# A hybrid attention layer on one core: rotated half tiles split into high and low parts, joined by 64 small transfers, and x by rows loaded behind a weight chunk

## What is computed

```
u    = rms_norm(x, attn_pre_g)
proj = u @ w_in                      # 1024 x 1952: MLA latents (416), then MoBA q, k, v (512 each)
mla_o  = mla_attention(...)          # 8 heads, causal, 64 + 32 (rotary) dims
q, k   = rope(moba q), rope(moba k)  # 8 heads of 64: x1*cos - x2*sin | x2*cos + x1*sin
moba_o = moba_attention(q, k, v)     # blocks of 256; with 512 tokens: causal softmax attention
h = x + rms_norm(concat(mla_o, moba_o) @ w_out, attn_post_g)
h = h + rms_norm(square(relu(rms_norm(h, mlp_pre_g) @ w_up)) @ w_down, mlp_post_g)
```

## Time and profile before

| | |
|---|---|
| median of 3 runs | 562.42 us (562.3 to 562.56) |
| the profiled execution | 562.25 us |
| its span in the trace | 560.5 us |
| TensorE busy | 548.9 us, 98% |
| VectorE, ScalarE, GpSimd busy | 392.2, 293.4, 92.2 us |
| granted TensorE clock | 0.998 of full |
| DMA | 99.66 MB, 178 GB/s on average |

### The profile page before, as it was taken

One profiled execution on the slowest core, in us unless ns is written; L12 is line 12 of the kernel. 1 busy time (PEld: TensorE's weight loads), 2 busy tenths in 40 slices (PEclk: granted clock), 3 DMA queues, 4 the chain that ended last, 5 costly groups with the idle time before them and its releaser, 6 DMA issues.

```text
span 560.5 us, 7840 instructions
## 1 busy us (share of the span) xinstructions
PE 548.9 (98%) x2730; PEld 451.9 (81%) x2730; DVE 392.2 (70%) x745; ACT 293.4 (52%) x612; POOL 92.2 (16%) x152
## 2 busy tenths in 40 slices
PE   9999999999999999999999999999999999999994
PEld 8888898876656888988888888888888888888883
DVE  5359473487785366367766775779777989778897
ACT  6563172688884364463344335344465656656561
POOL 1263110355784012200000000000000001000003
PEclk9999999999999999999999999999999999999999
DMA  8933652000002940387778886787975565605403
GB/s 289 370 123 104 201 165 76 0 2 2 0 2 76 340 149 1 108 297 272 229 277 279 278 283 229 276 279 265 357 280 195 181 216 167 219 21 204 150 1 150
DMA packets 43454, 99.66 MB, mean 178 GB/s; under 512 B 3232, under 2 KB 20896, under 8 KB 40096
## 3 DMA queue, kind: packets, MB, share of 16 engines
q1 hardware_dynamic: 42992, 98.54, 51.0%
q10 hardware_dynamic: 432, 0.74, 0.4%
HBM read 81.44 MB, written 15.73 MB: 173 GB/s over the span
## 4 chain that ended last, share of the span: by engine, by line
PE 91%; DMA 3%; DVE 2%; POOL 2%; ACT 1%; issue 1%; ACTq 0%; DVEq 0%; POOLq 0%
PE bank L1327 28%; PE bank L1328 27%; PE bank L1329 27%; PE bank L1539 3%; PE bank L1558 3%; POOL probs L527 1%; DMA w_raw<-in_w_in 1%; DMA x_raw<-in_x_cols 1%; PE bank L1504 1%; DVE w_lo L883 1%; PE bank L1333 1%; DVE bank L1000 1%; ACT w_hi L575 1%; ACT probs L665 0%; PE bank L1463 0%
## 5 line engine op out<-in xcount | busy, mean ns | idle before, releaser
L1327 PE MATMUL bank<-uT_hi,w_hi 128*128 128x512 f32 (+1 forms) x344 | 129.3, 376 | 0.8 <-DVE w_lo L883 0.8
L1328 PE MATMUL bank<-uT_lo,w_hi 128*128 128x512 f32 (+1 forms) x344 | 128.8, 374 | 0.0
L1329 PE MATMUL bank<-uT_hi,w_lo 128*128 128x512 f32 (+1 forms) x344 | 128.7, 374 | 0.0
L1327 PE MATMUL bank<-w_hi,a_hi 128*128 128x512 f32 x224 | 87.2, 389 | 0.0
L1329 PE MATMUL bank<-w_hi,a_lo 128*128 128x512 f32 x224 | 87.2, 389 | 0.0
L1328 PE MATMUL bank<-w_lo,a_hi 128*128 128x512 f32 x224 | 87.1, 389 | 0.0
L883 DVE SCALAR_TENSOR_TENSOR w_lo<-w_raw,g_up,w_hi 128x256 fp32r<-128x256 f32 x128 | 52.1, 480 | 48.4 <-ACT w_hi L575 48.4
L575 ACT ACTIVATE w_hi<-w_raw,g_up 128x256 fp32r<-128x256 f32 x128 | 53.0, 496 | 45.6 <-PE bank L1329 24.8
L1327 PEld LDWEIGHTS bank<-uT_hi,w_hi 128*128 128x128 f32 x344 | 64.7, 188 | 12.9 <-issue 1.1
L1328 PEld LDWEIGHTS bank<-uT_lo,w_hi 128*128 128x128 f32 x344 | 64.8, 188 | 11.5
L1329 PEld LDWEIGHTS bank<-uT_hi,w_lo 128*128 128x128 f32 x344 | 64.7, 188 | 11.4
(11 more groups left out here) (161 smaller groups left out, 871.3 us busy)
## 6 DMA issues: line engine op xcount, KB each, us to landing
stage<-in_w_down SPq DMA_DIRECT2D x17, 1024.0 KB, 4.9
w_raw<-in_w_up SPq DMA_DIRECT2D x16, 1024.0 KB, 8.4
pair_sums<-stage SPq DMA_DIRECT2D x13, 1024.0 KB, 9.9
w_raw<-in_w_down SPq DMA_DIRECT2D x10, 1024.0 KB, 6.7
w_raw<-pair_sums SPq DMA_DIRECT2D x10, 1024.0 KB, 4.8
w_raw<-in_w_in SPq DMA_DIRECT2D x6, 1024.0 KB, 7.5
w_raw<-in_w_out SPq DMA_DIRECT2D x4, 1024.0 KB, 4.8
stage<-pair_sums SPq DMA_DIRECT2D x3, 1024.0 KB, 4.8
```

The costliest lines, as they stand in the source:

```text
L1327: nc.tensor.matmul(out, lh, rh, start=start, stop=False)
L1328: nc.tensor.matmul(out, lh, rl, start=False, stop=False)
L1329: return nc.tensor.matmul(out, ll, rh, start=False, stop=stop)
```

## The change

- On SyncE, the four loads of x by rows (`x_sb`) wait until chunk 2 has landed (`raw_in[0]` at 32). Everything behind them in the queue waits with them.
- A rotated half tile in `rt1` is split: ScalarE writes its high part to a new tile `half_hi`, VectorE puts the low part in place into `rt1`. For queries this stands after chunk 5 on both engines, for keys before chunk 7.
- SyncE joins both: `join_hi(0)` (16 transfers), KV chunk, `join_lo(0)` (16), chunks 6 and 7, `join_hi(1)`, `join_lo(1)` (32), into `mq_hi`, `mq_lo`, `mk_hi`, `mk_lo`, which replace `mqT` and `mkT`.
- Turning a key tile waits for the low parts of the query tile (`lo_in`) instead of the query pieces. The MLA query rotation uses the second half of `rt2` instead of `rt1`, and no longer waits for key pieces.
- Pair scores are three passes (hi x hi, hi x lo, lo x hi), the two heads in turn within each pass, 6 instructions for a tile.
- TensorE waits for all 16 arrivals before it transposes the first probabilities; before it waited for 8 at the same place.

```diff
@@ -113,8 +113,8 @@
         wo_lo = [sb(f"wo_lo{i}", [P, CW], F32R, stack=att) for i in range(2)]
-        mqT = sb("mqT", [P, HEADS // 2, S], stack=att)
-        mkT = sb("mkT", [P, HEADS // 2, S], stack=att)
+        mq_hi = sb("mq_hi", [P, HEADS // 2, S], F32R, stack=att)
+        mq_lo = sb("mq_lo", [P, HEADS // 2, S], F32R, stack=att)
         with ExitStack() as start:
@@ -136,9 +136,13 @@
         pT = [sb(f"pT{i}", [P, TRI], stack=att) for i in range(4)]
+        with ExitStack() as halves:
+            half_hi = sb("half_hi", [P, NT, HW], F32R, stack=halves)
         with ExitStack() as cols:
...
         probs += [sb(f"probs{i}", [P, TRI], stack=att) for i in (2, 3)]
+        mk_hi = sb("mk_hi", [P, HEADS // 2, S], F32R, stack=att)
+        mk_lo = sb("mk_lo", [P, HEADS // 2, S], F32R, stack=att)
         att.close()
@@ -346,14 +351,23 @@
-            def half_tiles(which):
-                for j in range(NT):
-                    g, s = j // 2, j % 2
-                    sp.wait_ge(roped, NT * which + j + 1)
-                    for h in range(HEADS // 2):
-                        r0 = MOBA_D * (h % 2) + 32 * s
-                        sp.dma_start((mqT, mkT)[which][r0:r0 + 32, 2 * g + h // 2, :],
-                                     rt1[32 * h:32 * h + 32, j, :]).then_inc((mq_in, mk_in)[which][j], 16)
+            def join(n, parts, src, arrived):
+                j = n % NT
+                g, s = j // 2, j % 2
+                for h in range(HEADS // 2):
+                    r0 = MOBA_D * (h % 2) + 32 * s
+                    sp.dma_start(parts[n // NT][r0:r0 + 32, 2 * g + h // 2, :].bitcast(F32),
+                                 src[32 * h:32 * h + 32, :]).then_inc(arrived[n], 16)
+
+            def join_hi(which):
+                for n in range(NT * which, NT * which + NT):
+                    sp.wait_ge(half_h, n + 1)
+                    join(n, (mq_hi, mk_hi), half_hi[:, n % NT, :].bitcast(F32), hi_in)
+
+            def join_lo(which):
+                for n in range(NT * which, NT * which + NT):
+                    sp.wait_ge(half_l, n + 1)
+                    join(n, (mq_lo, mk_lo), rt1[:, n % NT, :], lo_in)
@@ -370,6 +384,7 @@
             in_chunk(2)
+            sp.wait_ge(raw_in[0], 32)
             for t in range(NT):
@@ -381,11 +396,13 @@
             chunk(Q_CH, w_q_v, 2 * HEADS * QH)
-            half_tiles(0)
+            join_hi(0)
             chunk(KV_CH, w_mla_kv_up.rearrange("o p n -> p o n"), HEADS * P)
+            join_lo(0)
             in_chunk(6)
             in_chunk(7)
-            half_tiles(1)
+            join_hi(1)
+            join_lo(1)
             for i, r in enumerate(OUT_CH):
@@ -631,7 +648,15 @@
                 hi_part(kT_hi[i][NOPE:QH, :], ps[3][0:ROPE, :]).then_inc(krh, 1)
+            def half_parts(which):
+                for n in range(NT * which, NT * which + NT):
+                    act.wait_ge(roped, n + 1)
+                    if n >= NT:
+                        act.wait_ge(hi_in[n - NT], 64)
+                    hi_part(half_hi[:, n % NT, :], rt1[:, n % NT, :]).then_inc(half_h, 1)
+
             in_hi(5)
+            half_parts(0)
             arrived(Q_CH)
@@ -644,6 +669,7 @@
                 hi_part(v_sb[:, 0, t, :], ps[t][:, :]).then_inc(v_ready, 1)
+            half_parts(1)
             in_hi(7)
@@ -951,7 +977,7 @@
                 if n >= NT:
-                    dve.wait_ge(mq_in[j], 64)
+                    dve.wait_ge(lo_in[j], 64)
                 if n >= 2:
@@ -967,7 +993,14 @@
                 lo_part(kT_lo[i][NOPE:QH, :], ps[3][0:ROPE, :], kT_hi[i][NOPE:QH, :]).then_inc(krl, 1)
+            def half_parts(which):
+                for n in range(NT * which, NT * which + NT):
+                    dve.wait_ge(half_h, n + 1)
+                    whole = rt1[:, n % NT, :]
+                    lo_part(whole.bitcast(F32R), whole, half_hi[:, n % NT, :]).then_inc(half_l, 1)
+
             in_lo(5)
+            half_parts(0)
             dve.wait_ge(wh_ready, Q_CH + 1)
@@ -978,12 +1011,10 @@
             dve.wait_ge(roped, 2 * NT)
-            for j in range(2):
-                dve.wait_ge(mk_in[j], 64)
             for t in range(NT):
...
                 q4 = q_nat[:, t, :].rearrange("p (h c) -> p h c", c=QH)[:, :, NOPE:QH].rearrange("p h (s d) -> p h s d", s=2)
-                m1 = rt1[:, t % 2, 0:HEADS * ROPE].rearrange("p (h s d) -> p h s d", h=HEADS, s=2)
+                m1 = rt2[:, t % 2, HEADS * ROPE:].rearrange("p (h s d) -> p h s d", h=HEADS, s=2)
                 m2 = rt2[:, t % 2, 0:HEADS * ROPE].rearrange("p (h s d) -> p h s d", h=HEADS, s=2)
@@ -1498,13 +1530,14 @@
                     w, tok = P * (t + 1), slice(P * t, P * t + P)
-                    for h in range(2):
-                        b, c = PAIR_AT[t][h]
-                        r = slice(MOBA_D * h, MOBA_D * h + MOBA_D)
-                        last = nc.tensor.matmul(ps[b][:, c:c + w], mqT[r, m - FIRST, tok], mkT[r, m - FIRST, 0:w],
-                                                start=True, stop=True)
-                        if t != 2:
-                            last.then_inc(s_full, 1)
+                    for n, (q, k) in enumerate(((mq_hi, mk_hi), (mq_hi, mk_lo), (mq_lo, mk_hi))):
+                        for h in range(2):
+                            b, c = PAIR_AT[t][h]
+                            r = slice(MOBA_D * h, MOBA_D * h + MOBA_D)
+                            last = nc.tensor.matmul(ps[b][:, c:c + w], q[r, m - FIRST, tok], k[r, m - FIRST, 0:w],
+                                                    start=n == 0, stop=n == 2)
+                            if n == 2 and t != 2:
+                                last.then_inc(s_full, 1)
@@ -1581,7 +1614,7 @@
-            for arrived in mq_in + mk_in:
+            for arrived in hi_in + lo_in:
                 pe.wait_ge(arrived, 64)
```

More of the change, by code:

```diff
@@ L205, in build @@
         kT_full, kh, kl = sem("kT_full"), sem("kh"), sem("kl")
-        mq_in, mk_in = [[sem(f"{n}{j}_in") for j in range(NT)] for n in ("mq", "mk")]
+        hi_in, lo_in = [[sem(f"half_{n}{j}_in") for j in range(2 * NT)] for n in ("hi", "lo")]
+        half_h, half_l = sem("half_h"), sem("half_l")
         turn_in, r_full, r_ready = sem("turn_in"), sem("r_full"), sem("r_ready")
```

## The result

The changed kernel takes **566.64 us** (median of 6, 566.31 to 569.16) against 562.41 (median of 6, 561.75 to 562.59) of the kernel before beside it: ratio 1.0083, 95% interval 1.0065 to 1.0101. Its profiled execution took 566.95 us with a span of 565.2. The forecast time, 566.5, is met. How it comes about is only in part what the prediction says, as the trace shows.

The account below looks back on a forecast made before the run. TensorE, busy 548.9 of 560.5 us, was taken to bound the kernel. The terms +5.3, -0.8 and -0.4 on 562.25 gave 566.35, against the median 566.5 us; range 563.3 to 570.0.

Parts of the forecast that it names:

- Part 1: Loading x by rows behind weight chunk 2: booked as a gain, -0.8 us, bounds -0.8 and 0.
- So I take 16 us for its landing.: Chunk 2 without x beside it was to land at 16 us instead of 18.8, removing TensorE's 0.79 us loss.
- Chunk 3's landing, "26.9" to "29": Chunk 3 of w_in, queued behind the delayed x, was to land between 26.9 and 29 us.
- So it may land up to 29.3.: Latest harmless landing of chunk 3, given its splitting times and TensorE needing it at 34.8 us.
- Part 2: 64 joining transfers instead of 32 on SyncE delay chunk 6, so TensorE starts group 3 late: +5.3 us.
- The landing: Chunk 6 of w_in, with chunk 7 started 0.4 us behind it, was taken to land after 7.0 us.
- the forecast 86.0: Start of group 3 on TensorE: forecast at 86.8 instead of 81.53, before Part 1's 0.8 us gain.
- The stall before the value products: TensorE idle 4 to 5 us after the query up-projection, waiting for a copy behind chunk 6's high half.
- The sum: Whole kernel: gain of Part 1, loss of Part 2 and gain of Part 3 added, from 562.25 to 566.35 us.
- Part 3: Pair scores in three passes: long block 2.00 to about 1.7 us, mostly becoming waiting; -0.4 us for four rounds.
- the rival of 571.9: Pair scores: the high/low passes of two heads don't overlap, rounds grow by 5.0 us; 571.9 us, chance 10%.
- the covers: Slack before further stalls: 0.7 us before chunk 7, 2.9 us for the last key parts.

Follow-up runs that it names:

- e2: The kernel before with only the wait ahead of x by rows added: 565.88 us, ratio 1.0067.
- e9: The kernel of e2 with chunk 3 asked for ahead of x by rows, both behind the wait: 563.64 us, ratio 1.0023.
- e1: The changed kernel without its wait ahead of x by rows: 567.45 us, ratio 1.0077.
- e4: The changed kernel without its wait and with chunk 6 asked for ahead of the low parts' joins: 562.77 us, ratio 1.0011.
- e5: The changed kernel without its wait, joins of query tiles 2 and 3 started from ScalarE's queue: 561.48 us, ratio 0.9990.
- e6: The kernel of e4 with pair scores as plain f32 products of the high parts alone: 563.63 us, ratio 1.0023.
- e8: The kernel before with pair scores in three passes, operands split after the 32 old joining transfers: 561.90 us, ratio 0.9990.
- e3: The changed kernel, wait kept, with chunk 6 asked for ahead of the low parts' joins: 566.21 us, ratio 1.0072.
- e7: The kernel of e2 with 40 extra bf16 matmuls on TensorE in the idle time ahead of group 2: 565.96 us, ratio 1.0061.

## Why the prediction met the time, and where its steps failed

**Part 1 failed, in three steps.**
- *"So I take 16 us for its landing."* Chunk 2 landed at 18.4, after 7.6 us (7.8 with x beside it). With or without x it takes the same, so x isn't what made it slow, and it has a thin end. The stretches from 15 to 19 us of the changed kernel (columns as above, all engines' busy times between):

```profile
15.00:16.00 1.00, 1.00 (x7) 1.00 (x6) 1.00 (x2) 0.00 (x0) 0.00 (x0) 1.00 0.74 279
16.00:17.00 1.00, 1.00 (x8) 0.99 (x7) 0.02 (x1) 0.00 (x0) 0.00 (x0) 1.00 0.33 121
17.00:18.00 1.00, 1.00 (x7) 0.98 (x6) 0.00 (x0) 0.00 (x0) 0.00 (x0) 1.00 0.13 51
18.00:19.00 1.00, 1.00 (x7) 0.98 (x6) 0.00 (x0) 0.50 (x1) 0.00 (x0) 1.00 0.01 2
```

  Before, with x queued behind it, the share in the same four stretches was 1.15, 0.90, 1.02 and 0.99. The wait turns it into idle time of the DMA engines, for a gain of 0.3 at chunk 2's split (18.50 instead of 18.83). The idle 0.79 ahead of 24.31 became 0.59, not nothing.
- *Chunk 3's landing, "26.9" to "29".* It started 4.7 later and took 9.4: 31.3, past even the 29.3 that the prediction allows (its own terms, 34.8 - 2.56 - 2.74, give 29.5); hence the idle 1.04 at 36.67.
- *"So it may land up to 29.3."* This is the costly one. The cover was measured against TensorE, which wants chunk 3 at 34.8. But ScalarE's split of chunk 3 stands ahead of the latents' squares, and on them hang GpSimd's statistics, VectorE's scaling, its split of chunk 4 and the turned queries, that is, group 2. The prediction names that chain in the next sentence ("VectorE's chain there hangs on chunk 3") and gives it no number. Its slack was 0.06 us: in the kernel before, VectorE's turn that frees the first banks ends at 47.81 + 0.68 = 48.49, and group 2 starts at 48.55:

```profile
47.81 0.68 DVE L958 TENSOR_TENSOR rt<-bank,turn 128x512 f32<-128x512 f32 x1
...
48.55 0.50 PE L1327 MATMUL bank<-uT_hi,w_hi 128*128 128x512 f32 x1
```

  Each microsecond of the split of chunk 3 is a microsecond of the end: 3.6 later in e2 costs 3.5, 1.45 later in e9 costs 1.4. Booked was -0.8.

**Part 2: the mechanism is right, shown by e1, e4 and e5.** Starts of 0.590, joins 54.17 to 75.7, chunk 6 at 75.72 against 74.0 less 0.8. Of these 2.5 us, 1.8 are there at the first transfer, most of it (1.5 against e1) because the wait delayed ScalarE's queue instead of advancing it, and 0.7 are the line of starts. The landing was mis-sized the other way, 5.5 us instead of 7.0. So group 3 starts at 87.10 against the forecast 86.0, by errors of +1.8, +0.7 and -1.5. The stall before the value products, with part 1 taken away, is 3.3 us (e1), near the +3.5 that the prediction gives for a landing of 5.2, and the rest of e1's +5.1 is mostly the half clock. In the changed kernel 0.2 of this stall is left.

**The sum failed.** The terms were added as if in series. They meet at one point, the first copy of the query up-projection, and there the later counts: +3.5 (e2) and +5.1 (e1) give together +4.2, not 8.6. The later was the chain by way of chunk 6, by 0.2; TensorE's own lateness, 3.7 and 1.6 of the half clock, lay beneath it. Part 1's error, some 4 us the wrong way, stayed invisible in the total for that reason. Had the two delays been in series, the time would have been near 571, outside the range. The agreement of 566.5 with 566.6 is in part luck: one delay hid the other, and three errors nearly cancelled. (The forecast's own range is said to begin at 563.6; its terms, landing 5.2 and starts 0.59, add up to 563.3.)

**Part 3 is right in size and kind:** -0.53 against -0.4, with the long block's gain turned into a wait for GpSimd of 0.34 to 0.36 in three of four rounds. The passes of the two heads overlap; the rival of 571.9 falls, by the rows of the second round and by e6, where plain products are 0.56 slower and not 5 faster.

**What was borne out of the covers:** the last key parts landed in time, and no stall came before chunk 7. **What was missing:** the half clock. The trace of before has no idle time of TensorE over 0.8 us in this stretch, and the prediction, which forecast one of 4 to 5 us, put no price on what the clock does behind it; in e1 that was 1.6 us.

## What to carry to other kernels

When a transfer is moved, follow every instruction that stands behind its consumer on the consumer's engine, not only the last reader of its data, and write the slack of that chain as a number; here it was 0.06 us, where the one that the prediction reckoned with let chunk 3 land up to 29.3, 1.6 us after it did. Delays that meet at one instruction are to be compared, not added: take each away alone and both together before any is declared harmless. And before a store is doubled in transfers, look whether the split can be made behind them: in e8 two instructions of 128 x 2048 on each engine, one for queries and one for keys, did what 32 more starts of 0.59 us did, in time that was idle anyway.

## What the runs showed of the hardware that was not expected

- A chunk of 1 MB queued behind other transfers ended thinly here (chunk 2 of the changed kernel): the DMA share falls from 0.74 to 0.33, 0.13 and 0.01 in the last three microseconds before it has landed. A wait for this landing left the DMA engines idle; in the kernel before, with x queued behind, the share in the same stretches was 0.90 to 1.15.
- Behind an idle time of 2.6 to 3.3 us TensorE's granted clock fell to the half (1.2 instead of 2.4 GHz) for about 3 us in some executions and not in others: passes at 0.43 in the changed kernel (idle 2.58) and in e1 (3.29), at 0.23 in e2 (2.62) and e3 (2.59). Over whole executions the mean granted clock was 0.993 or 0.994 in all six of the changed kernel, 0.991 to 0.996 in e1, which varied by 4.3 us, and 0.995 to 0.998 in the kernel before, which has no such gap. That the idle time is the cause is likely but not shown: one execution of e5 (0.86 idle in its trace) and one of e7 (the gap filled) also had 0.993, and neither has a trace.
- Transfers of 64 KB started from ScalarE's queue land in 2.0 us like SyncE's, but in 5.9 when chunks 6 and 7 are in flight beside them (e5, low parts); started on SyncE's queue behind chunk 6 they took 3.2 (e4).
